# Expert blocks of 120 slots, and gate and up weights as two halves by columns

## What is computed

```
def hier_moe(xn, ...):                       # 1088 rows of 1024
    # top-1 group of 4, then top-2 of its 8 experts: 2176 (token, expert) pairs over 32 experts
    ...
    def expert_block(args):
        xblk, e = args
        hid = jax.nn.silu(xblk @ w_gate[e]) * (xblk @ w_up[e])    # 1024 x 256 each
        return hid @ w_down[e]                                    # 256 x 1024
    ...
    return jnp.zeros_like(xn).at[tok_buf].add(yb * w_buf[:, None])
```

## Time and profile before

| | |
|---|---|
| median of 3 runs | 1304.73 us (1304.19 to 1305.5) |
| the profiled execution | 1305.92 us, of which the profiler's span is 1304.3 us |
| PE busy | 1258.5 us (96% of the span) |
| VectorE busy | 1037.1 us (80%) |
| ScalarE busy | 705.7 us (54%) |
| the expert loop | about 1016 to 1304 us of the span |

### The profile page before, as it was taken

One profiled execution on the slowest core, in us unless ns is written; L12 is line 12 of the kernel. 1 busy time (PEld: TensorE's weight loads), 2 busy tenths in 40 slices (PEclk: granted clock), 3 DMA queues, 4 the chain that ended last, 5 costly groups with the idle time before them and its releaser, 6 DMA issues. The chain is left out here.

```text
span 1304.3 us, 28488 instructions
## 1 busy us (share of the span) xinstructions
PE 1258.5 (96%) x11224; PEld 839.1 (64%) x11224; DVE 1037.1 (80%) x1479; ACT 705.7 (54%) x1160; POOL 309.2 (24%) x280
## 2 busy tenths in 40 slices
PE   7999999989999999999999999999998999999996
PEld 5456666656666666666666666654554888888884
DVE  5678777774858999999999686644757899999993
ACT  4656666654244333523441474433311899999993
POOL 1273111110001100110100000000034266676662
PEclk9999999998799999999999999999999999999998
DMA  8700000022214415432442116538578899999992
GB/s 330 177 12 4 1 0 0 8 114 77 42 50 110 115 42 139 107 84 72 116 109 84 50 50 220 184 104 333 193 270 301 275 393 390 394 390 386 394 312 50
DMA packets 53082, 211.36 MB, mean 162 GB/s; under 512 B 14560, under 2 KB 15776, under 8 KB 40416
## 3 DMA queue, kind: packets, MB, share of 16 engines
q1 hardware_dynamic: 31888, 156.95, 32.1%
q0 software_dynamic: 18672, 44.42, 14.0%
q10 hardware_dynamic: 2448, 8.98, 1.7%
HBM read 180.98 MB, written 39.72 MB: 169 GB/s over the span
## 5 line engine op out<-in xcount | busy, mean ns | idle before, releaser
L1348 DVE SCALAR_TENSOR_TENSOR big<-c_region,c_taps,big 128x1024 f32<-128x1024 f32 (+1 forms) x120 | 153.9, 1282 | 3.7 <-ACT caT L1044 3.7
L74 PE MATMUL c_psb<-xnT,w_taken 128*128 128x364 f16 x456 | 145.8, 320 | 0.0
L76 PE MATMUL c_psb<-xnT,f_w_l 128*128 128x364 f16 x456 | 145.7, 320 | 0.0
L75 PE MATMUL c_psb<-xnT,w_taken 128*128 128x364 f16 x456 | 145.7, 320 | 0.0
L1348 DVE SCALAR_TENSOR_TENSOR caT<-c_region,c_taps,caT 128x1024 f32<-128x1024 f32 x112 | 143.6, 1282 | 0.0
L2041 POOL DMA_INDIRECT y_all<-o_hn,e_idx_y x29 | 91.9, 3168 | 41.4 <-POOL e_idx_y L2037 23.3
L74 PE MATMUL c_psa<-xnT,w_taken 128*128 128x364 f16 x312 | 99.1, 318 | 0.1
L76 PE MATMUL c_psa<-xnT,f_w_l 128*128 128x364 f16 x312 | 99.0, 317 | 0.0
L75 PE MATMUL c_psa<-xnT,w_taken 128*128 128x364 f16 x312 | 99.0, 317 | 0.0
L74 PE MATMUL o_psH<-big,e_gu 128*128 128x128 f16 x512 | 87.4, 219 | 0.8 <-DVE big L2388 0.8
L75 PE MATMUL o_psH<-big,e_gu 128*128 128x128 f16 x512 | 87.4, 219 | 0.0
(11 more groups left out here) (410 smaller groups left out, 3922.0 us busy)
## 6 DMA issues: line engine op xcount, KB each, us to landing
e_gu<-w_gu SPq DMA_DIRECT2D x28, 1024.0 KB, 14.4
w_taken<-w_feat SPq DMA_DIRECT2D x48, 512.0 KB, 3.9
e_d<-w_dn SPq DMA_DIRECT2D x15, 1024.0 KB
o_room<-w_gu SPq DMA_DIRECT2D x12, 1024.0 KB
xnT<-w_gu SPq DMA_DIRECT2D x12, 1024.0 KB
big<-w_gu SPq DMA_DIRECT2D x12, 1024.0 KB, 18.5
c_region<-gates POOLq DMA_DIRECT2D x8, 1092.0 KB, 5.7
xnT<-w_dn SPq DMA_DIRECT2D x6, 1024.0 KB
```

What stands on the lines that cost most here:

```text
L74: pe.matmul(out, stat[0], mov[0], start=start, stop=False)
L75: pe.matmul(out, stat[0], mov[1], start=False, stop=False)
L76: return pe.matmul(out, stat[1], mov[0], start=False, stop=stop)
L1348: dve.scalar_tensor_tensor(y_j, glu[:, p, j:j + SEQ], tap, y_j, op0=ALU.mult, op1=ALU.add).then_inc(tap_done, 1)
```

## The change

Blocks have 120 slots: the moving operand of the 96 matmuls of `gate_up`, the transposed rows, the hidden rows and the result have 120 columns or rows in place of 128. The transfers by index keep 128 rows, the last 8 of them always out of bounds. As 120 is no power of two, the block number of a pair comes from a multiplication and a shift. Up to 18 extra blocks are provided for in place of 16. The two halves of the gate and up weights are no longer chunks 0 to 3 and 4 to 7 of both, but the gate weights (half 0) and the up weights (half 1), each still 1 MB in one transfer of the same shape. PE waits for half 1 only before the up product, ACT's cut of half 0 waits for the gate product alone, and the order inside both bodies is another. In the diff the first `body` is ScalarE's and the second VectorE's; `gate_up` is TensorE's.

```diff
-BLK = 128
-NOV = 16
+BLK = 120
+NOV = 18
...
-LANES, LANE_BITS = 4, 5
+LANES = 4
+LANE = BLK // LANES
+PER_LANE, PER_LANE_BITS, LANES_BITS = 2185, 16, 2
...
-        psY = psH[:, 1]
+        psY = psH[0:BLK, 1]
+        psRows = psT[:, :, 0:BLK]
...
             def load_up(b, f, half, used=0):
-                sp.dma_start(gu32[f][:, halves[half]], A[("w_gu0", "w_gu1")[half]][b].rearrange("p (k n) -> p k n", k=HK)
+                sp.dma_start(gu32[f][:, half], A[("w_gate", "w_up")[half]][b].rearrange("p (k n) -> p k n", k=KC)
                              ).then_inc(gu_ld[f][half], 16)
...
             def body(b, p, up, down, u, first=False):
                 gate(b, p)
-                act.wait_ge(gu_mm, b + 1)
                 cut(up, p, 0)
                 if not first or p:
                     result(b - 1, 1 - p, u if p else u - 1, first)
+                hidden(b)
                 rows(b + 2, p)
-                hidden(b)
+                act.wait_ge(gu_mm, b + 1)
                 cut(up, p, 1)
                 if not first or p:
                     cut_down(down, 1 - p)
...
             def body(b, p, up, down, first=False):
+                low(b + 2, up, p, 0)
                 gate(b, p)
-                low(b + 2, up, p, 0)
+                hidden(b)
                 rows(b + 2, p)
-                hidden(b)
                 low(b + 2, up, p, 1)
                 if not first:
                     low_down(b + 1, down, 1 - p)
...
             def gate_up(b, p, first=False, part=range(4)):
                 if part[0] == 0:
                     pe.wait_ge(gu_low[0], b + 1)
-                    pe.wait_ge(gu_low[1], b + 1)
                     pe.wait_ge(xT_low, b + 1)
...
                 for j in part:
-                    cols = slice(j * P, (j + 1) * P)
+                    if j == 2:
+                        pe.wait_ge(gu_low[1], b + 1)
+                    cols = slice(j % 2 * P, (j % 2 + 1) * P)
```

More of the change, by code:

```diff
@@ L1725, in ffn_phase @@
         xg = xnT_f[:, rest:rest + 2 * D].rearrange("p (a n) -> p a n", a=2)
-        sg, hid = (xnT_f[:, rest + 2 * D + i * DE:rest + 2 * D + (i + 1) * DE].rearrange("p (k n) -> p k n", k=2) for i in range(2))
+        sg, hid = (xnT_f[:, rest + 2 * D + i * DE:rest + 2 * D + (i + 1) * DE].rearrange("p (k n) -> p k n", k=2)[:, :, 0:BLK]
+                   for i in range(2))
         hT = xnT_f[:, rest + 2 * D + 3 * DE:rest + 2 * D + 4 * DE].bitcast(F16).rearrange("p (a k n) -> p a k n", a=2, k=2)
-        hT_h, hT_l = hT[:, 0], hT[:, 1]
-        lastT_h, lastT_l = (big_f[:, rest:rest + 2 * D].bitcast(F16).rearrange("p (b a k n) -> p b a k n", b=2, a=2, k=KC)[:, a, 0, 0:2]
+        hT_h, hT_l = hT[:, 0, :, 0:BLK], hT[:, 1, :, 0:BLK]
+        lastT_h, lastT_l = (big_f[:, rest:rest + 2 * D].bitcast(F16).rearrange("p (b a k n) -> p b a k n", b=2, a=2, k=KC)[:, a, 0, 0:2, 0:BLK]
                             for a in range(2))
         xT = big_f[:, rest:rest + 2 * D].bitcast(F16).rearrange("p (b a k n) -> p b a k n", b=2, a=2, k=KC)
-        xT_h, xT_l = xT[:, 0], xT[:, 1]
+        xT_h, xT_l = xT[:, 0, :, :, 0:BLK], xT[:, 1, :, :, 0:BLK]
         pairs = big_f[:, rest + 2 * D:rest + 2 * D + 2 * NBLK].rearrange("p (b a) -> p b a", a=2)
@@ L1745, in ffn_phase @@
         room = sb("o_room", [P, W_GU + W_DN], F32)
-        gu32.append(room[:, 0:W_GU].rearrange("p (k n) -> p k n", k=KC))
+        gu32.append(room[:, 0:W_GU].rearrange("p (a k n) -> p a k n", a=2, k=KC))
         d32.append(room[:, W_GU:].rearrange("p (k n) -> p k n", k=2))
@@ L1866, in weight @@
         def weight(b):
-            return pairs[:, ds(b, 1), 1]
+            return pairs[0:BLK, ds(b, 1), 1]
         def rounds(eng):
@@ L2102, in cut @@
                 act.wait_ge(gu_ld[f][half], need)
-                act.activation(gu_h[:, p, halves[half]], gu32[f][:, halves[half]], ACT.Copy,
+                act.activation(gu_h[:, p, half], gu32[f][:, half], ACT.Copy,
                                scale=S_W).then_inc(gu_high[half], 1)
@@ L2112, in rows @@
                 act.wait_ge(xT_done, b + 1)
-                act.activation(xT_h[:, p], psT[:], ACT.Copy, scale=S_X).then_inc(xT_high, 1)
+                act.activation(xT_h[:, p], psRows, ACT.Copy, scale=S_X).then_inc(xT_high, 1)
             def gate(b, p):
@@ L2134, in result @@
                     act.wait_ge(y_st[p], 16 * u)
-                act.activation(y_o[:, p], psY, ACT.Copy, scale=weight(b)).then_inc(y_out, 1)
+                act.activation(y_o[0:BLK, p], psY, ACT.Copy, scale=weight(b)).then_inc(y_out, 1)
             def body(b, p, up, down, u, first=False):
                 gate(b, p)
-                act.wait_ge(gu_mm, b + 1)
                 cut(up, p, 0)
@@ L2346, in control_groups @@
                 dve.wait_ge(l_mm, TT)
[L2347 to L2350, removed]
+                done(dve.tensor_scalar(cnt[:, 0], psC[0:1], 1.0, float(BLK - 1), ALU.max, ALU.add))
+                done(dve.tensor_scalar(cnt_i[:, 0:NE], cnt[:, 0], float(PER_LANE), None, ALU.mult))
+                done(dve.tensor_scalar(cnt_i[:, 0:NE], cnt_i[:, 0:NE], PER_LANE_BITS + LANES_BITS, None, ALU.arith_shift_right))
+                done(dve.tensor_scalar(cnt[:, 0], cnt_i[:, 0:NE], 1.0, None, ALU.subtract))
                 done(dve.tensor_tensor_scan(cnt[:, 1], one[:], cnt[:, 0], 0.0, ALU.mult, ALU.add))
@@ L2376, in low @@
                 dve.wait_ge(gu_high[half], b + 1)
-                dve.scalar_tensor_tensor(gu_l[:, p, halves[half]], gu32[load[0]][:, halves[half]], S_W,
-                                         gu_h[:, p, halves[half]], op0=ALU.mult,
+                dve.scalar_tensor_tensor(gu_l[:, p, half], gu32[load[0]][:, half], S_W,
+                                         gu_h[:, p, half], op0=ALU.mult,
                                          op1=ALU.subtract).then_inc(gu_low[half], 1)
@@ L2503, in keep_warm @@
                 for i in range(n):
-                    pe.matmul(psH[:, 1, 512:D], gu_h[:, 0, i % KC, 0:P], gu_h[:, 0, i % KC], start=True, stop=True)
+                    pe.matmul(psH[:, 1, 512:D], gu_h[:, 0, 0, i % KC, 0:P], gu_h[:, 0, 0, i % HK * 2:i % HK * 2 + 2], start=True, stop=True)
             def turn_h(t):
@@ L2743, in in_turn @@
         return w.reshape(NG, EPG, P, -1).transpose(1, 0, 2, 3).reshape(NE, P, -1)
-    gu = in_turn(np.concatenate([w_gate, w_up], 2).reshape(NE, KC, P, 2 * DE).transpose(0, 2, 1, 3))
+    gate, up = (in_turn(w.reshape(NE, KC, P, DE).transpose(0, 2, 1, 3)) for w in (w_gate, w_up))
     dn = in_turn(w_down.reshape(NE, 2, P, D).transpose(0, 2, 1, 3))
```

33 lines of the change are left out of this document (16 added, 17 removed).

## The result

The changed kernel took 1343.78 us, the median of 4 runs (1339.89 to 1344.89), and the kernel before 1304.65 us in 4 runs beside it (1304.19 to 1305.5): a ratio of 1.0294, with a 95% interval of 1.028 to 1.0307, so 2.9% slower. The forecast was 1341.6 us, with a range of 1329 to 1348. The profiled execution of the changed kernel took 1339.89 us, of which the span is 1338.2.

A forecast was written before the change was run, and what follows sets the result against it. PE was taken to bound the kernel before, with DVE, ACT and DMA close; after the change, a DVE-ACT loop of waits. Span 1304.3 + 36.3 + 4.3 - 3.7 = 1341.2 us, forecast median 1341.6, range 1329 to 1348.

The forecast's parts named there:

- The loop: Expert loop: seven dependent DVE and ACT terms from hid to hid make 10.15 us a lap, +36.3 us over 28 laps; chance 0.84.
- PE: Expert loop: 120-column matmuls take 52.3 ns, PE's lap falls from 8.83 to 8.44 us, and PE idles 1.7 us ahead of down.
- The rival of the slower clock: PE in the expert loop: granted clock falls to 1.2 GHz for good, lap 16.9 us, +189 us, 1530 us; chance 0.02.
- The start: Before the loop: low of block 2's half 0 delays hid(0) to 1020.39 and hid(1) to 1028.34, +4.3 us.
- The end: Last blocks, hid(29) to down(31): shorter by 0.97, 0.87 and 1.82 us, together -3.7 us.
- The faster rival: Expert loop: DVE doesn't bind, waits stay covered, and full DMA engines limit the saving to about 4.4 us: 1300 us; chance 0.04.

The follow-up runs named there:

- experiment 4: Changed kernel with rows ahead of hidden again on ACT and DVE, low of half 0 still ahead of hid: 1316.58 us, ratio 1.0093.
- experiment 10: Changed kernel with DVE's low of half 0 moved behind rows (hid, hidden, rows, low, low, low_down), ACT as changed: 1319.57 us, ratio 1.012.
- experiment 3: Changed kernel with one DVE line moved, hid ahead of low of half 0; hidden stays ahead of rows on both engines: 1305.19 us, ratio 1.0012.
- experiment 2: Kernel before (128 slots, halves by chunks) with only the new order on ACT and DVE: 1344.18 us, ratio 1.0304.
- experiment 1: Changed kernel with the old order in both bodies; 120 slots and halves by columns stay: 1305.13 us, ratio 1.0006.
- experiment 8: Kernel before with only the halves by columns and the later wait for half 1; 128 slots, old order: 1303.87 us, ratio 1.0001.
- experiment 9: Changed kernel loading only the first half of the down weights from block 7 on: 1343.89 us, ratio 1.0303.
- experiment 7: Changed kernel with 128 slots and 16 extra blocks again; new order and halves by columns stay: 1344.67 us, ratio 1.0309.
- experiment 5: 120 slots and halves by columns in the old order, loading only half of the down weights from block 7 on: 1295.57 us, ratio 0.9933.
- experiment 6: Kernel before, loading only the first half of the down weights from block 7 on: 1303.83 us, ratio 0.9999.

## Why the prediction was right

**The loop.** This step held, term by term: forecast 10.15 us and 28 laps of it, 284.2 us; measured 10.14 and 283.86. The parts are to be seen in the rows: 0.43 us from hid to ACT's hidden (1106.34 to 1106.77), 0.31 to rows, 0.85 to the second cut, 1.94 to DVE's second low (1107.93 to 1109.87), then 2.21, 2.20 and 2.20. The experiments took single terms out, and the lap fell by what was taken: `rows` by experiment 4, the wait for the second cut by experiment 10, and everything down to PE's lap by putting an operation of 2.2 us behind hid again in experiment 3. One figure beside the sum was too large: DVE was to idle 1.74 us in a lap and idled 0.47 + 0.45 + 0.64 = 1.56. Each operation behind a wait loses the 0.08 to 0.09 us by which it otherwise starts ahead of the recorded end of the one before (1112.08, where 1109.87 + 2.29 is 1112.16), and two more of them stand behind a wait than before. The lap doesn't depend on this, since its terms go from start to start.

**Cause.** That it is the order and nothing else is shown from both sides: alone it costs 3.0% (experiment 2), and without it the rest of the change costs nothing (experiments 1 and 8).

**PE.** 52.3 ns a matmul was forecast and 52.5 measured; a lap of 8.44 us, and 8.46 measured where PE ruled. The Trainium skill, TensorE: Matmul & The Clock Gate, section "Wait — 56ns, not 53.3ns?", gives N / 2.4 GHz + about 2.5 ns for the distance of warm matmuls, which for 120 columns is an estimated 52.5 ns; the trace agrees. The step forecast PE's idle time as 1.7 us ahead of down, released by DVE's hidden. It was 1.50: the lap of 10.14 less 8.46 is 1.68, and 0.17 of it is the record of the last matmul of gate_up, 0.22 us long where the next one would start after 0.0525. The profile names another releaser; the time of DVE's hidden shows the link, not the name.

**The clock.** The rival of the slower clock did not come in the loop of the changed kernel: with 184.46 busy us of 216, and a gap of 1.5 us in each lap, the granted clock stayed at 1.00, which is 2.4 GHz. Behind longer gaps elsewhere it was lower in some executions. In the profile of experiment 1 PE was idle for 2.11 us ahead of a down at 1235.53, and the granted clock was 0.79 from 1234 to 1238 and 0.78 from 1238 to 1242, then 1.00 again. Experiment 3 had a gap of 2.26 us in this stretch at 1.00, and the same time, so this does not explain where experiment 1's gain went.

**Start and end.** The start was the term that could be read least well, since this execution came to the loop 2.7 us earlier than that of the earlier trace rows: DVE's `rows` of block 0 is at 1005.71, where it was at 1008.43. hid(0) stood at 1017.25, on the clock of before 1019.97, where 1020.39 was forecast. The end was 7.93 and 4.88 us from hid to hid (forecast 7.94 and 4.89) and 1.98 us from hid(31) to down(31) (forecast 1.88). From `rows` of block 0 to the end of the span it was 332.49 us in the changed kernel and 295.87 before: +36.6, and the sum of the three terms was +36.9. That it comes so close is in part luck: measured in the same way, the start was +3.9 (forecast +4.3), the loop +35.9 (+36.3) and the end -3.2 (-3.7). Of the end's miss 0.4 us lies behind down(31), in the last scatter's start to the end of the span, 9.46 us in place of 9.07; in the profiles of the experiments it was 9.3 to 9.5.

**The median.** It is 2.2 us over the forecast, and the terms of the loop don't hold this. The profiled execution of the changed kernel was the shortest of its four, 1.7 us under the forecast. Two stretches outside the loop vary between profiles. `rows` of block 0 is at 1005.7 to 1009.6 us, and was earliest in this one. And down(31) stands behind a gap on PE: from its first matmul to ACT's last `result` it is 2.93 us in the changed kernel, at a granted clock of 1.00, but 4.59 us in experiment 9, whose loop is the same, at a clock of 0.64. The timeline of ACT, the changed kernel's row first and then that of experiment 9:

```profile
1326.77 1.11 ACT L2138 ACTIVATE o_hn<-o_psH,big 120x1024 f32<-120x1024 f32 x1 [3.07 <-PE o_psH L78]
```

```profile
1330.53 1.11 ACT L2139 ACTIVATE o_hn<-o_psH,big 120x1024 f32<-120x1024 f32 x1 [4.73 <-PE o_psH L78]
```

Experiments 1 and 7 show the same (4.61 and 4.45 us, at 0.65 and 0.64), the others don't. PE had been idle for 2.71 us ahead of down(31) in the changed kernel and in experiment 9 alike. How the 2.2 us divide between the two stretches was not settled.

**The faster rival** was priced wrongly, though it did not decide. The step read 4.4 us of room off block 30 and let these through: 1300 us. The runs in which its condition holds, experiments 1 and 3, gained nothing. What failed was to read the room from one landing, that of a half of gate and up weights. The landings of the kernel before, 10.5, 15.7, 21.2 and 27.7 us, grew from lap to lap up to 1177 us already, so a shorter lap falls behind sooner: in experiment 1 SP's transfer instructions get longer from 1147.93 on, the buffers hide it from ACT until about 1200 us, then cuts of down weights wait as well, and the rate falls from 389 to 375 GB/s. The share of 1.02, from which the step took it that the DMA engines were full, is no sign of this: experiments 5 and 6 have it too, at 359 to 366 GB/s, and no engine waited for weights there.

## What to carry to other kernels

When two engines work in turn (one makes the high part, the other the low), write down once what follows on what from one lap to the next and add it up; if a long operation that needs nothing from the other engine stands just behind each hand-over, the loop is short, and moving it by one place can cost most of its length (here 10.14 - 8.45 = 1.69 us of 2.20). Before a faster engine is hoped for, look whether the transfers can follow. Neither the slack of one transfer nor a full share of the DMA engines tells; the time from issue to landing, followed over many laps, does: where it grows already, a faster engine brings little or nothing until less is moved.

## What the runs showed of the hardware

- Where transfers fall behind, the engine that issues them is held up. In experiment 1 one transfer instruction on SP took 8.45 us at 1197.55 and one 6.51 us at 1227.26; the same instructions take 0.33 to 0.36 us where there is room. The first long one is at 1147.93 (2.42 us), 52 us ahead of ACT's first wait for weights. The loads behind it are then issued late too. The timeline of SP in experiment 1:

```profile
1197.07 0.43 SPq L1892 DMA_DIRECT2D e_gu<-w_up  x1
1197.55 8.45 SPq L1898 DMA_DIRECT2D o_room<-w_dn  x1
...
1227.26 6.51 SPq L1973 DMA_DIRECT2D big<-w_up  x1
```

- The weight load of a tile with 120 columns takes longer than one with 128: the loads of down take 0.13 us with 120 columns, and took 0.10 us with 128 in the kernel before. It is hidden here, since down's matmuls start 0.22 us apart in both.
- A share of 1.02 of the DMA engines was seen at 359, 366 and 389 GB/s (experiments 6 and 5, and the kernel before), with landings that stayed at 8.0 to 11.7 us, rose from 12.4 to 18.1 us, and rose from 10.5 to 27.7 us.
- After the same gap of 2.71 us on PE the granted clock stayed at 1.00 over down(31) in one execution and was 0.64 in another, at a cost of 4.59 - 2.93 = 1.7 us.
